# Blocks of 336 instead of 320 columns for four split operands of a two-layer encoder step

## The chip, the cores and the metric

The kernel runs on one core of one Trainium2 chip. The metric is device microseconds of one execution, from the first to the last instruction and what the launch adds around it; the median of a few runs is compared.

## What is computed

Two layers of a streaming encoder are applied to 320 tokens at once (256 of a prompt and 64 of a sample with cached keys), model width 2048. In each layer, with RMS norms in front of each product:

```python
h = rms_norm(x, g_mix);  A, B, C, D = split(h @ w_in)      # four kinds of attention
x = x + concat(A, B, C, D) @ w_out
x = x + square(relu(rms_norm(x, g_mlp) @ w_up)) @ w_down   # 2048 -> 8192 -> 2048
x = x + (ple @ w_ple) * sigmoid(rms_norm(x, g_ple) @ w_ple_gate)
```

All values are float32, and the outputs must keep nearly float32 accuracy.

## The kernel before

Activations are kept feature-major: a tensor of width 2048 is 16 blocks of 128 features (one per partition), and each block holds the 320 tokens as 320 consecutive fp32 words of the partition. `KB` is 16 and `TOK` is 320.

**A product in three matmuls.** The big products run on the fast fp32r form of TensorE, which keeps fewer bits than fp32. Each operand is therefore split in an upper half and a remainder: weights into `whi` and `wlo`, activations into `xhi` and `xlo` (the normed x) or `hhi` and `hlo` (the MLP's activations after the squared relu). The helper `product` (lines 699 to 701) issues lower weight by upper activation, upper by lower, and upper by upper, all into the same PSUM bank:

```python
mm(out, lo[:, k, cols], xh, start=start, stop=False)
mm(out, hi[:, k, cols], xl, start=False, stop=False)
return mm(out, hi[:, k, cols], xh, start=False, stop=stop)
```

The weights are the stationary operand (128 by 128) and the activation block is the moving one (128 by 320). Every matmul therefore has its own weight load.

**Order.** `gemm_chunk` makes four blocks of outputs, a chunk: for 8 units of weights, for 4 output blocks `m`, for the 2 activation blocks `k` of the unit, one `product`. This is 8 x 4 x 2 x 3 = 192 matmuls. A unit is a 512 KB transfer into one of four slots of `ring`; ScalarE copies it to `whi` (line 1136), GpSimd subtracts to get `wlo` (line 662), TensorE waits for `lo_ready`. A layer's MLP is 4 groups of 4 up chunks (from `xhi`, `xlo`) and 4 down chunks (from `hhi`, `hlo`). Ahead of the MLP the last four blocks of `w_out` run the same way (4 times 48 matmuls, on `hhi` and a small tensor `hlast`), behind it `w_ple` (4 times 24 matmuls, on `pleh` and `plel`) and the gate (4 chunks, on `xhi` and `xlo`). VectorE takes the outputs out of PSUM, and makes `xhi` (line 1370), `xlo` (line 1373), `hhi` (line 1766 through the helper of line 1326) and `hlo` (line 1768). Everything else (`w_in`, attention, most of `w_out`) runs ahead of this in a layer, with other tensors. `w_in` has split products too (lines 760 to 763), but there the weights move and the activations are loaded; a unit holds two to four blocks of 256, 264, 288 or 512 weight columns, so that of 264 and of 288 the second block begins 32 and 128 bytes further modulo 256 than the first, and of 256 and 512 at the same place.

**Where the tensors lie.** Buffers are placed by hand in SBUF, many on top of others that are dead by then; all waits are explicit semaphores. A block of 320 words is 1280 bytes, five times 256, so all 16 blocks of a tensor begin at the same place modulo 256 bytes. Worked out from the list of allocations, relative to the first buffer: `xhi`, `hhi`, `whi` and `wlo` begin at 0 modulo 256, `xlo` at 64 (its placement says `+ 64`), `hlo` at 192, `hlast`, `pleh` and `plel` at 32. Weight slots are 4096 bytes and the 128 columns that a matmul loads are 512 bytes, so every weight load begins at 0 modulo 256.

Of the kernel before, what the change touches and what calls it, by code (L numbers as in the profile page):

```python
# [16 lines left out]
TOK = SEQ + DSEQ  # L17
# [6 lines left out]
KB = DM // 128  # L24
# [38 lines left out]
def build(nc, I, O):  # L63
# [4 lines left out]
    with ctx:  # L68
        f32r = mybir.dt.float32r
        top = [nc.sbuf_base + (-nc.sbuf_base) % 64]  # L70

        def sb(name, shape, dtype=f32, at=None):

            words = 1
            for n in shape[1:]:
                words *= n
            if at is None:
                at = top[0]
                top[0] += 4 * (words + (-words) % 8)
            return nc.alloc_sbuf_tensor_at(name, shape, dtype, offset=at)  # L80

        def sem(name):
            return ctx.enter_context(nc.semaphore(name))

        at = top[0]
        x = sb("x", [128, KB, TOK])
        proj_b = sb("proj_b", [128, 3, 1536], at=at)
        early = top[0]
        hid = sb("hid", [128, KB, TOK])
        hhi = sb("hhi", [128, KB, TOK], f32r, early)  # L90
        early += 4 * KB * TOK // 2
        xw = sb("xw", [128, KB, XW], f32r, early)
        xv = sb("xv", [128, KB, 256], f32r, early + 4 * KB * XW)
# [9 lines left out]
        at = top[0]  # L103
# [2 lines left out]
        vtok = sb("vtok", [128, 7, 256])  # L106
        prob = sb("prob", [128, 4, 960])
        probT = sb("probT", [128, 704])
        xhi = sb("xhi", [128, KB, TOK], f32r, at)
        xlo = sb("xlo", [128, KB, TOK], f32r, at + 4 * KB * TOK + 64)  # L110
        assert at + 8 * KB * TOK + 64 <= top[0]
        at = top[0]
        ring = sb("ring", [128, RING, 1024])
        rlo = sb("rlo", [128, RING, 1024], f32r, at)
        at = top[0]
# [6 lines left out]
        eps = sb("eps", [128, 1])  # L122
        at = top[0]
        arena = sb("arena", [128, KB * TOK])
        hlo = sb("hlo", [128, KB, TOK], f32r, at)
        proj_d = arena[:, 0:3 * 1544].rearrange("p (t n) -> p t n", t=3)
        plout = arena[:, :].rearrange("p (b n) -> p b n", b=KB)
        otok = sb("otok", [128, 3, 256])
# [17 lines left out]
        at = top[0]  # L146
# [1725 lines left out]
```

How the kernel before makes its waits and increments, by code:

```python
            def hold(s, value):  # L445
                sp.wait_ge(s, value)
                sp.sem_inc(sp_passed, 1)
# [1 line left out]
            def load(l, q4, u, dst_cols, src, tail=False):  # L450
                s = u % RING
                if tail:
                    sp.wait_ge(lo_ready, l * HL + N_WU + 4 * q4 + u + 1 - TAIL0 - RING)
                else:
                    sp.wait_ge(unit_used, l * UNITS + 4 * q4 + u + 1)
                dst = ring[:, s, 0:dst_cols]
                if len(src.shape) == 3:
                    dst = dst.rearrange("p (a n) -> p a n", a=src.shape[1])
                sp.dma_start(dst, src).then_inc(raw_loaded[s], 16)
# [7 lines left out]
            def first_loads(l):  # L468
                sp.wait_ge(half_free, l * CHUNKS + 2)
                for name, w in VECS:
                    src = I[name][l, :] if name != "lam_init" else I["lam_init"][l, :]
                    sp.dma_start(vec[:, VOFF[name]:VOFF[name] + w], src.partition_broadcast(128)).then_inc(vec_loaded, 16)
                with nc.allow_non_contiguous_dma("feature-major gains"):
                    for i, name in enumerate(("g_mlp", "g_ple")):
                        sp.dma_start(gains[:, 1 + i, :], I[name][l, :].rearrange("(a p) -> p a", p=128)).then_inc(vec_loaded, 16)
                sp.dma_start(flog[:, 0:4, :], I["cache_d_logf"][l, 0, :, :].rearrange("(t p) h -> p t h", p=128))\
                    .then_inc(fc_loaded, 16)
# [29 lines left out]
            def store(g, dst, src):  # L508
                sp.dma_start(dst, src).then_inc(stored[g], 16)
```

## Time and profile before

| | us |
|---|---|
| median of 3 runs | 3526.51 |
| lowest and highest | 3521.68, 3527.46 |
| the profiled execution's own time | 3529.45 |
| its span, first to last instruction | 3527.6 |
| TensorE busy in the span | 3359.4 |

The profiled execution took 3529.45 us, 2.94 us more than the median; 1.85 us of it lie outside the span. Times in the rows are microseconds from the span's start unless marked ns. PE is a matmul on TensorE, PEld a weight load (the two overlap), DVE VectorE, ACT ScalarE, POOL GpSimd. Matmuls are pipelined: a duration of 310 ns is from entry to exit, and what counts is the distance between the starts of two that follow each other. The mean granted TensorE clock is 0.969 of full speed.

### The profile page before, as it was taken

The page shows a single profiled execution, that of the slowest core. Times are in us where ns is not written, and L with a number is a line of the kernel's source. Part 1 is how long each engine was busy: PE and PEld are TensorE (multiplying, and loading weights), DVE is VectorE, ACT ScalarE, POOL GpSimd, SP SyncE. Part 2 cuts the span into 40 slices and gives each one's busy share as a digit, 9 for nine tenths or more (in the row PEclk, how much of TensorE's full clock was granted, in tenths as well). Part 3 has the DMA queues.
Part 4 walks back from the last instruction along what each step waited for, and adds up shares of the span by engine and source line. Part 5 has one row for each costly group of instructions (what it writes and reads, how often), then busy time and mean ns, then how long its engine had stood idle before and what let it go on. Part 6 is the DMA issues. An engine that isn't in the chain of part 4 may idle for free.

```text
span 3527.6 us, 60466 instructions
## 1 busy us (share of the span) xinstructions
PE 3359.4 (95%) x20676; PEld 3030.3 (86%) x20676; DVE 1280.4 (36%) x2301; ACT 1143.7 (32%) x1630; POOL 2261.2 (64%) x2989
## 2 busy tenths in 40 slices
PE   7998989999999999999989998999999999999998
PEld 5676756699999999999967776666999999999998
DVE  4324554464041130324352345445520513204153
ACT  3333332233333333333343332323333333333332
POOL 5554200188888898888865542003988988888886
PEclk9999999899999999999989999989999999999999
DMA  5333322145555455555454333223455554555544
GB/s 159 113 112 110 101 72 87 58 138 150 151 148 153 146 150 153 150 152 148 128 146 114 107 99 109 66 75 94 137 151 152 147 155 139 155 150 149 151 138 125
DMA packets 295723, 453.05 MB, mean 128 GB/s; under 512 B 36336, under 2 KB 111344, under 8 KB 294832
## 3 DMA queue, kind: packets, MB, share of 16 engines
q1 hardware_dynamic: 295328, 448.66, 43.2%
q8 instruction: 179, 2.93, 0.3%
q0 software_dynamic: 144, 0.87, 0.1%
q14 instruction: 72, 0.59, 0.1%
HBM read 435.54 MB, written 14.06 MB: 127 GB/s over the span
## 4 chain that ended last, share of the span: by engine, by line
PE 85%; DVE 6%; issue 4%; DMA 2%; ACT 2%; POOL 1%; SPq 1%; DVEq 0%; ACTq 0%; POOLq 0%
PE ps L700 19%; PE ps L701 19%; PE ps L699 19%; PE ps L797 5%; PE ps L785 5%; PE ps L760 4%; PE ps L763 4%; PE ps L762 3%; PE ps L889 1%; DMA ring<-in_w_in 1%; DVE xhi L1370 1%; PE ps L835 1%; PE ps L893 1%; PE ps L924 1%; PE ps L892 1%
## 5 line engine op out<-in xcount | busy, mean ns | idle before, releaser
L662 POOL TENSOR_TENSOR wlo<-ring,whi 128x256 fp32r<-128x256 f32 x2400 | 1836.5, 801 | 855.5 <-ACT whi L1136 855.0
L1136 ACT ACTIVATE whi<-ring 128x1024 fp32r<-128x1024 f32 x600 | 635.9, 1061 | 1380.6 <-PE ps L701 1380.6
L699 PE MATMUL ps<-xhi,wlo 128*128 128x320 f32 x2560 | 792.8, 310 | 11.2 <-POOL wlo L662 7.2
L700 PE MATMUL ps<-xlo,whi 128*128 128x320 f32 x2560 | 796.6, 311 | 0.0
L701 PE MATMUL ps<-xhi,whi 128*128 128x320 f32 x2560 | 792.9, 310 | 0.0
L701 PE MATMUL ps<-hhi,whi 128*128 128x320 f32 x2176 | 674.0, 310 | 0.0
L699 PE MATMUL ps<-hhi,wlo 128*128 128x320 f32 x2176 | 661.6, 304 | 4.7 <-DVE plel L1746 4.7
L648 POOL TENSOR_TENSOR rlo<-ring,whi 128x256 fp32r<-128x256 f32 (+2 forms) x576 | 421.0, 766 | 368.1 <-ACT whi L1120 367.8
L700 PE MATMUL ps<-hlo,whi 128*128 128x320 f32 x2048 | 629.9, 308 | 0.0
L699 PEld LDWEIGHTS ps<-xhi,wlo 128*128 128x128 f32 x2560 | 486.6, 190 | 14.3 <-issue 12.5
L700 PEld LDWEIGHTS ps<-xlo,whi 128*128 128x128 f32 x2560 | 484.3, 189 | 1.0 <-issue 0.4
L701 PEld LDWEIGHTS ps<-xhi,whi 128*128 128x128 f32 x2560 | 483.4, 189 | 0.0
L699 PEld LDWEIGHTS ps<-hhi,wlo 128*128 128x128 f32 x2176 | 410.4, 189 | 5.3 <-issue 5.1
L760 PE MATMUL ps<-rlo,xw 128*128 128x512 f32 (+3 forms) x1056 | 371.0, 357 | 44.4 <-DVE xw L1339 16.7
L701 PEld LDWEIGHTS ps<-hhi,whi 128*128 128x128 f32 x2176 | 410.2, 189 | 0.0
L1329 DVE TENSOR_TENSOR x<-ps,x 128x320 f32<-128x320 f32 x224 | 107.2, 488 | 797.5 <-PE ps L701 770.2
L700 PEld LDWEIGHTS ps<-hlo,whi 128*128 128x128 f32 x2048 | 383.0, 187 | 0.0
L763 PE MATMUL ps<-whi,xw 128*128 128x512 f32 (+3 forms) x1056 | 362.3, 349 | 0.0
L760 PEld LDWEIGHTS ps<-rlo,xw 128*128 128x128 f32 x1056 | 204.5, 194 | 78.6 <-issue 54.7
L762 PE MATMUL ps<-whi,xv 128*128 128x512 f32 (+3 forms) x704 | 248.0, 352 | 0.0
L785 PE MATMUL ps<-hid,ring 128*128 128x320 f32 x768 | 230.5, 457 | 6.9 <-ACT vtok L1179 3.0
L1120 ACT ACTIVATE whi<-ring 128x1024 fp32r<-128x1024 f32 (+2 forms) x152 | 147.5, 974 | 263.7 <-DMA ring<-in_w_in 223.5
(246 smaller groups left out, 3198.0 us busy)
## 6 DMA issues: line engine op xcount, KB each, us to landing
ring<-in_w_up SPq DMA_DIRECT2D x256, 512.0 KB, 3.7
ring<-in_w_down SPq DMA_DIRECT2D x256, 512.0 KB, 3.8
ring<-in_w_in SPq DMA_DIRECT2D x120, 512.0 KB, 3.6
ring<-in_w_out SPq DMA_DIRECT2D x64, 512.0 KB, 3.8
ring<-in_w_ple_gate SPq DMA_DIRECT2D x64, 512.0 KB, 3.8
xsave<-x SPq DMA_DIRECT2D x8, 640.0 KB, 5.5
x<-xsave SPq DMA_DIRECT2D x8, 640.0 KB, 5.0
ring<-in_w_in SPq DMA_DIRECT2D x16, 288.0 KB, 2.8
```

The costliest lines, as they stand in the source:

```text
L648: last = nc.gpsimd.tensor_tensor(rlo[:, s, c:c + w], ring[:, s, c:c + w], whi[:, s, c:c + w].bitcast(f32), ALU.subtract)
L662: last = nc.gpsimd.tensor_tensor(wlo[:, s, c:c + LO_COLS], ring[:, s, c:c + LO_COLS], whi[:, s, c:c + LO_COLS].bitcast(f32), ALU.subtract)
L699: mm(out, lo[:, k, cols], xh, start=start, stop=False)
L700: mm(out, hi[:, k, cols], xl, start=False, stop=False)
L701: return mm(out, hi[:, k, cols], xh, start=False, stop=stop)
L760: mm(out, head, lo[:, k, :], start=(kk == 0), stop=False)
L762: mm(out, xv[:, kk, t * 128:(t + 1) * 128], hi[:, k, :], start=False, stop=False)
L763: last = mm(out, head, hi[:, k, :], start=False, stop=(kk == KB - 1))
L785: last = mm(ps[:, out_bank(b), 0:TOK], w[:, k - k0, c:c + 128], hid[:, k, :], start=(k == k0), stop=(k == k1 - 1))
L797: return nc.tensor.transpose(out, in_, ident[0:in_.shape[0], 0:in_.shape[0]])
L1120: A(whi[:, s, 0:nk * ncol], ring[:, s, 0:nk * ncol], ACT.Copy).then_inc(hi_ready, 1)
L1136: A(whi[:, s, :], ring[:, s, :], ACT.Copy).then_inc(hi_ready, 1)
```

## The change

A constant `PITCH = TOK + 16` is added, and `xhi`, `xlo`, `hhi` and `hlo` are allocated with blocks of 336 words of which 320 are used. A block is then 1344 bytes, 5 x 256 + 64: each block begins 64 bytes further modulo 256 than the one before it, and every fourth block at the same place. `xlo` moves up with the longer `xhi` and begins again 64 modulo 256; the other three begin where they did. Each tensor is 1024 bytes longer per partition. `x`, `hid`, the weights, `hlast`, `pleh` and `plel`, all instructions, their order, shapes and waits are as they were.

```diff
+        PITCH = TOK + 16
         at = top[0]
         x = sb("x", [128, KB, TOK])
...
-        hhi = sb("hhi", [128, KB, TOK], f32r, early)
+        hhi = sb("hhi", [128, KB, PITCH], f32r, early)[:, :, 0:TOK]
...
-        xhi = sb("xhi", [128, KB, TOK], f32r, at)
-        xlo = sb("xlo", [128, KB, TOK], f32r, at + 4 * KB * TOK + 64)
-        assert at + 8 * KB * TOK + 64 <= top[0]
+        xhi = sb("xhi", [128, KB, PITCH], f32r, at)[:, :, 0:TOK]
+        xlo = sb("xlo", [128, KB, PITCH], f32r, at + 4 * KB * PITCH + 64)[:, :, 0:TOK]
+        assert at + 8 * KB * PITCH + 64 <= top[0]
...
-        hlo = sb("hlo", [128, KB, TOK], f32r, at)
+        hlo = sb("hlo", [128, KB, PITCH], f32r, at)[:, :, 0:TOK]
```

## Rows read from the trace of the kernel before

**Rows 1.** The page, part 1: busy time, share and instructions of each engine.

```profile
PE 3359.4 (95%) x20676; PEld 3030.3 (86%) x20676; DVE 1280.4 (36%) x2301; ACT 1143.7 (32%) x1630; POOL 2261.2 (64%) x2989
```

**Rows 2.** The page, part 4: the chain that ended last, by line.

```profile
PE ps L700 19%; PE ps L701 19%; PE ps L699 19%; PE ps L797 5%; PE ps L785 5%; PE ps L760 4%; PE ps L763 4%; PE ps L762 3%; PE ps L889 1%; DMA ring<-in_w_in 1%; DVE xhi L1370 1%; PE ps L835 1%; PE ps L893 1%; PE ps L924 1%; PE ps L892 1%
```

**Rows 3.** Windows of each layer's split products: length, busy by engine, granted clock, DMA.

```profile
699.45:1769.65 1070.20, 1059.12 (x7218) 1055.94 (x7216) 334.95 (x475) 351.11 (x339) 914.74 (x1196) 0.99 0.50 148
2440.58:3510.40 1069.82, 1058.33 (x7218) 1055.17 (x7216) 334.73 (x475) 351.07 (x339) 915.07 (x1196) 0.99 0.50 146
```

**Rows 4.** The page, part 5: groups of matmuls by operand; count, busy time, mean ns.

```profile
L700 PE MATMUL ps<-xlo,whi 128*128 128x320 f32 x2560 | 796.6, 311 | 0.0
L701 PE MATMUL ps<-xhi,whi 128*128 128x320 f32 x2560 | 792.9, 310 | 0.0
L701 PE MATMUL ps<-hhi,whi 128*128 128x320 f32 x2176 | 674.0, 310 | 0.0
L700 PE MATMUL ps<-hlo,whi 128*128 128x320 f32 x2048 | 629.9, 308 | 0.0
```

**Rows 5.** Timeline of TensorE in a down chunk: start, duration, operands.

```profile
1342.94 0.30 PE L699 MATMUL ps<-hhi,wlo 128*128 128x320 f32 x1
1343.08 0.31 PE L700 MATMUL ps<-hlo,whi 128*128 128x320 f32 x1
1343.22 0.31 PE L701 MATMUL ps<-hhi,whi 128*128 128x320 f32 x1
1343.37 0.30 PE L699 MATMUL ps<-hhi,wlo 128*128 128x320 f32 x1
...
1344.24 0.30 PE L699 MATMUL ps<-hhi,wlo 128*128 128x320 f32 x1
```

**Rows 6.** Tiles hhi and hlo: matmul durations, ns least/median/most.

```profile
L699 PE MATMUL ps<-hhi,wlo x2176: 302/303/615, 699.5 to 3379.2; 128*128 128x320 f32 x198
L701 PE MATMUL ps<-hhi,whi x2176: 304/309/468, 700.1 to 3379.5; 128*128 128x320 f32 x198
L700 PE MATMUL ps<-hlo,whi x2048: 307/308/315, 852.9 to 3379.3; 128*128 128x320 f32 x187
```

**Rows 7.** Windows of whole chunks, TensorE alone: length, busy (count), granted clock, DMA.

```profile
1020.42:1077.03 56.61, 56.61 (x386) 1.00 0.50 149
1638.72:1652.80 14.08, 14.08 (x98) 1.00 0.42 132
...
2536.40:2591.87 55.47, 55.47 (x386) 1.00 0.52 151
...
2759.50:2816.10 56.60, 56.60 (x386) 1.00 0.51 149
2843.89:2927.05 83.16, 83.16 (x578) 1.00 0.52 153
...
3454.90:3510.36 55.46, 55.46 (x386) 1.00 0.33 100
```

**Rows 8.** Windows in w_in's products of 256, 264, 288 and 512 columns, TensorE alone.

```profile
73.36:88.58 15.22, 15.22 (x128) 1.00 0.89 262
345.03:348.56 3.53, 3.53 (x31) 1.00 0.15 24
391.25:400.95 9.70, 9.70 (x75) 1.00 0.38 96
1787.31:1808.86 21.55, 21.55 (x96) 1.00 0.60 151
```

**Rows 9.** The waits: who waited for whom, us in total, times, longest.

```profile
ACT whi L1136 <- PE ps L701: 1380.6, 576, 6.7
POOL wlo L662 <- ACT whi L1136: 855.0, 404, 283.0
```

**Rows 10.** Groups by line and form: VectorE's splitting of x; count, busy, mean ns.

```profile
L1373 DVE SCALAR_TENSOR_TENSOR xlo<-x,gains,xhi 128x320 fp32r<-128x320 f32 x64 | 56.5, 922 | 1.1
L1370 DVE TENSOR_SCALAR xhi<-x,gains 128x320 fp32r<-128x320 f32 x64 | 44.2, 731 | 0.3
```

## The prediction

> **What bounds the kernel now.** I began with the busy times. TensorE works in 3359.4 of 3527.6 us, the next engine, GpSimd, in 2261.2 [rows 1], and the chain that ended last is TensorE's for 85% of the span, with 57% on the three lines of `product`, 699 to 701 [rows 2]. All operands that the change moves are read by these lines, so the windows came next, cut to where they run: 1070.20 us in the first layer and 1069.82 in the second, together 61% of the span, TensorE busy in 99% of it and the granted clock 0.99 [rows 3]. Nothing starves it there. ScalarE's split of the weights waits for TensorE (1380.6 us), and GpSimd waits for ScalarE (855.0 us) [rows 9]. So the stage lasts as long as 7200 matmuls a layer at the pace at which TensorE passes from one to the next, and the question is whether that pace depends on where a moving block begins.
>
> The timeline says that it depends on the operands. In a down chunk three matmuls of one shape, with all data there, start 0.14, 0.14 and 0.15 us after each other, and after three rounds the pattern has moved by 1.30 us, 433 ns a round [rows 5]. Durations give the steps more finely. They are 303 ns for `hhi` with `wlo`, 308 for `hlo`, 309 for `hhi` with `whi` [rows 6]; if the step to the next matmul differs as the duration does, then 3s + 5 + 6 = 433.3, and the steps are about 140.7, 145.7 and 146.7 ns.
>
> Whole chunks show levels. A window's count includes matmuls in flight at its start (two here), so the chunk's own number, 192, is the divisor. Three down chunks: 83.16 us / 576 = 144.4 ns. The last two gate chunks: 55.46 / 384 = 144.4. Two up chunks of the first layer's second group: 56.61 / 384 = 147.4, and of the second layer's second group 56.60, the same; yet two up chunks of the second layer's first group run at 55.47 / 384 = 144.5. `w_ple`, whose halves and blocks all begin at one place modulo 256, takes 14.08 / 96 = 146.7 [rows 7]. The clock is granted at 1.00 in all these, the 2.4 GHz level, and DMA share is no guide (0.33 at 144.4, 0.50 at 147.4). So one program, on one placement, runs at 144.4 in most chunks and at 147.4 in others, and stays on a level for a whole chunk.
>
> For the sum, 14,400 matmuls split as follows. `w_ple` (192) is not moved, and of the rest I put 23 of 74 chunks' worth at 147.4 (the last three up chunks of seven of the eight groups, in which the same windows give 147.4 as in the two shown, and two for the uneven start of the first layer) and 51 at 144.4. The mean is 145.3.
>
> **The change part by part.** It issues the same instructions, waits and DMAs, and no queue is passed. Three things could differ.
>
> TensorE's reads. 2 x 2560 + 2560 + 2 x 2176 + 2048 = 14,080 matmuls read a moved tensor [rows 4]; 1 ns on each is 14.1 us. Of the three steps in a round, two pass between an upper half and its remainder, 64 bytes apart modulo 256. Only the third, from `hhi` of one block to `hhi` of the next, joins places that are equal modulo 256 and will be 64 bytes apart. In the down chunk it is the longest, 146.7 against a mean of 143.2 of the others. Made equal to them it saves 3.5 ns a round, 1.2 ns a matmul, 16 us. The trace has a nearest case of blocks that are offset, in `w_in`. Pace, less one column per cycle of 2.4 GHz: 256 columns 15.22 us / 127 - 106.7 = 13.2 ns, 512 columns 21.55 / 95 - 213.3 = 13.5, both without offset; 264 columns, 32 bytes between blocks, 3.53 / 29 - 110.0 = 11.7; 288 columns, 128 bytes, 9.70 / 73 - 120.0 = 12.9 [rows 8]. Offsetting blocks there gave between 0.3 and 1.8 ns a matmul, 4 to 25 us on 14,080. I take 0.85 ns, 12 us, the lower part of that, because the 264 run is only 29 matmuls long and the round in the down chunk may give back elsewhere what one step saves. The bounds are wider. Below: every step as short as the shortest, 140.7, would give (145.3 - 140.7) x 14,080 = 65 us. Above: every chunk at 147.4 costs 51 x 192 x 3.0 = 29 us.
>
> One rule speaks against any of this. The Trainium skill, "SBUF — State Buffer", section "Who interferes with whom", gives PE two independent read ports (one for the moving operand, one for weight loads) and says that PE and ACT never wait on anyone; by it the place of a block costs nothing and the sum would be 0. The steps of 140.7 to 146.7 ns and the two levels disagree with it, as far as they come from the places; that they do is inferred, not shown. A second page of the Trainium skill, "TensorE: Matmul & The Clock Gate", section "Wait — 56ns, not 53.3ns?", has bf16 matmuls follow each other at N / 2.4 GHz + 2.5 ns, which by an estimate would be 135.8 ns here and 134 us less; no row comes near.
>
> VectorE's and ScalarE's writes into the four tensors. Splitting x takes 56.5 + 44.2 us in all [rows 10], and `xhi` L1370 has 1% of the chain [rows 2], ahead of the first up chunk and the gate. Slices keep 320 consecutive words, so I take 0; a tenth of what is on the chain, 35 us, would be 3.5 us either way. Elsewhere VectorE's idle time (335 of 1070 us busy [rows 3]) covers it.
>
> Overlays. `hlo` now reaches 1024 bytes into `otok`, and `hhi`'s last block onto `kext`; both are used in attention, which is over by then, and no wait was added. Cost 0, and without that cover it would be a wrong value, not time.
>
> Sum: 3529.45 - 12 = 3517.5 for the profiled execution, which lies 2.94 above the median, so 3514.5 by the median, say 3515.
>
> **Rivals.** *Forecast, small gain*: 0.3 to 2 ns a matmul, 3498 to 3522. The upper figure includes that the 147.4 level goes too (23 x 192 x 3.0 = 13 us).
>
> *No change*: only the distance between an upper half and its remainder counts, and it is kept (64 and 192 modulo 256). For it: 264 and 288 columns differ little from 256 and 512. Against: levels change with nothing but what ran before. Time 3520 to 3533. The rule of "SBUF — State Buffer" in the Trainium skill, above, would give the same.
>
> *Slower*: the round of three that settles at 144.4 needs that all blocks begin alike. With the change, places repeat only after six matmuls within a unit (two blocks), and the next unit begins 128 bytes further, so the round is broken at each block. Then the pace is that of `w_ple`, 146.7: 51 x 192 x 2.3 - 23 x 192 x 0.7 = 22.5 - 3.1 = +19 us, 3546; or the upper level, +29, 3556. For it: 147.4 is held through whole up chunks at the same place in both layers, so the good round is not the only one the placement allows. Against: in `w_in` offset blocks never cost more than equal ones. It decides from a mean pace of 145.8, 0.5 ns above now.
>
> *Large gain*: most steps fall towards 140.7, 2.5 ns or more a matmul, 3463 to 3491. For it: that step recurs in every round of the down chunks. Against: no three in a row are so short.
>
> **How the numbers follow.** Chances: small gain 0.36, no change 0.25, slower 0.32, large gain 0.07. This kernel's runs lie within 0.2% of each other (5.8 us of 3526.5), so 0.2%, 7 us, is about what tells a change. Of the small gain a few hundredths end inside that, and as many of "no change" outside, so faster 0.43, same 0.25, slower 0.32. The forecast's own range is 3498 to 3522. For 8 in 10, the range must reach the slower cases up to 3548 (0.10 beyond) and down to 3485 (0.06 beyond).
>
> **What would show it.** Windows on down chunks: 192 matmuls in under 27.7 us for the forecast, 28.2 for the slower rival, 27.0 for a large gain. Up chunks of the middle groups at 27.9 us or less instead of 28.3. In the timeline the third step shorter than now. Stages outside the split products, and the waits of ScalarE and GpSimd per unit, as before. I am wrong if down chunks become slower while up chunks don't move, if the time moves in a stage with no split products, or if VectorE's splits lengthen.

## The result and the profile after

The change costs 16.5 us. Six runs of the kernel before have a median of 3525.26 us (3521.33 to 3533.01), six of the changed kernel 3541.78 (3537.44 to 3546.93): 1.0044 times, with a 95% interval of 1.003 to 1.0059. The profiled execution of the changed kernel took 3546.93 us with a span of 3545.1, 17.5 more than the span before.

The page after, part 1: busy time, share and instructions of each engine. Line numbers after are one higher, so `product` is 700 to 702.

```profile
PE 3374.4 (95%) x20676; PEld 3046.2 (86%) x20676; DVE 1288.5 (36%) x2301; ACT 1143.5 (32%) x1630; POOL 2254.4 (64%) x2989
```

The same instructions run on every engine [rows 1]. TensorE is busy 15.0 us longer, VectorE 8.1; ScalarE and GpSimd are no slower. The same windows of the layers' split products as in [rows 3], in the changed kernel (length, busy by engine, granted clock, DMA share, GB/s):

```profile
699.43:1780.40 1080.97, 1067.65 (x7218) 1064.29 (x7216) 341.17 (x475) 351.16 (x339) 911.79 (x1196) 0.99 0.49 146
2450.83:3528.02 1077.19, 1066.63 (x7218) 1063.73 (x7216) 335.19 (x475) 351.13 (x339) 911.72 (x1196) 0.99 0.49 145
```

They are 10.77 and 7.37 us longer, 18.1 in all. So the whole loss lies here, at the same mean granted clock. TensorE's own work in them is 8.53 and 8.30 us longer; its idle time changes by 2.2 and -0.9 us, so it is not starved either. VectorE is busy 6.2 us more in the first layer and 0.5 in the second, and the first layer's surplus is one instruction. The first of VectorE's 64 splits into `xhi` took 7.55 us, where the longest took 0.91 before (ns least/median/most, first and last start):

```profile
L1371 DVE TENSOR_SCALAR xhi<-x,gains x64: 374/857/7545, 708.2 to 3431.1; 128x320 fp32r<-128x320 f32 x64
```

It ended at 715.8, and GpSimd's first stretch of subtractions ran without a pause from 696.14 to 715.58; that VectorE waited for GpSimd is inferred from this. TensorE then stood idle for 5.01 us before 723.21, the granted clock over 714.53 to 730.34 was 0.78, a part of it at the lower of its two levels, 1.2 GHz (1.00 over the same stretch before), and the first up matmul began 38.0 us into the window instead of 34.2. So some 3.8 of the first layer's 10.77 us are a late start and not pace. One other kernel below has such a split, of 7.67 us: the one with x alone in blocks of 336. In the other fourteen traces none is over 0.96 us. No trace shows whether other executions of the changed kernel have it.

What is longer in ScalarE's and GpSimd's queues is waiting, as the waits after show against [rows 9]:

```profile
ACT whi L1137 <- PE ps L702: 1401.7, 577, 11.2
POOL wlo L663 <- ACT whi L1137: 880.7, 406, 283.6
```

ScalarE waits 21 us longer for TensorE, GpSimd 26 us longer for ScalarE: they stand behind a slower TensorE. Next the windows of whole chunks, TensorE alone, as in [rows 7]:

```profile
1025.73:1081.94 56.21, 56.21 (x387) 1.00 0.50 150
1110.16:1194.72 84.56, 84.56 (x578) 1.00 0.51 150
1648.50:1662.58 14.08, 14.08 (x99) 1.00 0.39 125
...
2547.37:2603.58 56.21, 56.21 (x387) 1.00 0.51 149
2773.30:2829.51 56.21, 56.21 (x387) 1.00 0.51 150
...
3471.70:3528.02 56.32, 56.32 (x386) 1.00 0.32 97
```

Read row by row, divided by the chunks' own matmuls: up chunks of the first layer's second group 56.21 / 384 = 146.4 ns (147.4 before); three down chunks 84.56 / 576 = 146.8 (144.4 before), 28.2 us a chunk, which is the sign that the prediction named for the slower rival; `w_ple`, not moved, 14.08 as before; up chunks of the second layer's first group 146.4 (144.5 before) and of its second group 146.4 (147.4 before); the last gate chunks 56.32 / 384 = 146.7 (144.4 before). Both levels of before are gone. In their place are paces of 146.4 to 146.8, between them and nearer to the upper.

That gives the sum. 32 chunks read `hhi` and `hlo` alone (2048 x 3 / 192): 32 x 192 x 2.4 ns = +14.7 us. 40 read `xhi` and `xlo`; with 21 of them at 147.4 and 19 at 144.4 their mean was 146.0, and 0.4 ns more in 32 up chunks and 0.7 in 8 gate chunks is +2.5 + 1.1 = 3.6 us. Together 18.3, against 16.8 of longer work and 18.1 of longer windows; the split 21 to 19 is an estimate of the prediction, and the windows hold the late start beside the pace.

The timeline of a down chunk after (start, duration, operands), against [rows 5]:

```profile
1120.71 0.31 PE L700 MATMUL ps<-hhi,wlo 128*128 128x320 f32 x1
...
1121.59 0.31 PE L700 MATMUL ps<-hhi,wlo 128*128 128x320 f32 x1
```

Two rounds of three take 0.88 us, 440 ns a round instead of 433. Averaged over the starts of all down chunks in the traces (pauses of 200 ns and more left out), the three steps of a round were 140.2, 145.1 and 148.3 ns; they are 147.5, 147.5 and 145.6. The third is 2.7 ns shorter, as forecast, and the two others are 7.3 and 2.4 longer. The tiles' durations (ns least/median/most) agree, against [rows 6]:

```profile
L700 PE MATMUL ps<-hhi,wlo x2176: 304/310/633, 699.4 to 3395.7; 128*128 128x320 f32 x198
L702 PE MATMUL ps<-hhi,whi x2176: 302/309/468, 700.1 to 3396.0; 128*128 128x320 f32 x198
...
L701 PE MATMUL ps<-hlo,whi x2048: 303/309/318, 856.2 to 3395.8; 128*128 128x320 f32 x187
```

The medians were 303, 309 and 308; they are 310, 309 and 309. The short one of the three is gone. The matmuls became alike, as forecast, but near the length of the long ones.

### The profile page after: what moved, and what is told of

It reads as the page before. It is cut to its first block, busy times and chain, and to the rows that moved or that the text cites. A ratio compares the mean times of both kernels' runs of the same rounds, so it can differ in the third digit from the quotient of the medians.

```text
span 3545.1 us, 60466 instructions
## 1 busy us (share of the span) xinstructions
PE 3374.4 (95%) x20676; PEld 3046.2 (86%) x20676; DVE 1288.5 (36%) x2301; ACT 1143.5 (32%) x1630; POOL 2254.4 (64%) x2989
## 4 chain that ended last, share of the span: by engine, by line
PE 85%; DVE 6%; issue 4%; ACT 2%; DMA 2%; POOL 1%; SPq 1%; DVEq 0%; POOLq 0%; ACTq 0%
PE ps L700 19%; PE ps L701 19%; PE ps L702 19%; PE ps L798 5%; PE ps L786 5%; PE ps L761 4%; PE ps L764 4%; PE ps L763 3%; PE ps L890 1%; DMA ring<-in_w_in 1%; DVE xhi L1371 1%; PE ps L925 1%; PE ps L894 1%; PE ps L836 1%; PE ps L893 1%
## 5 line engine op out<-in xcount | busy, mean ns | idle before, releaser
L700 PE MATMUL ps<-hhi,wlo 128*128 128x320 f32 x2176 | 677.5, 311 | 2.3 <-DVE plel L1747 2.3
```

## The experiments

Places below are bytes modulo 256, relative to where every weight load begins; a pair such as (0, 64) is the place of the upper half and that of the remainder. Before, x lies at (0, 64) and the MLP's activations, h for short, at (0, 192). In the change both run through four places, x through (0, 64), (64, 128), (128, 192), (192, 0), and h through (0, 192), (64, 0), (128, 64), (192, 128).

Three families of causes were set against each other: something other than the places (the longer tensors, their overlays), the distances between the moving blocks, and the place of a moving block against the weight loads that run beside the matmuls. The expectations letter them; here they are told in words. Unless said otherwise, each fence below is that kernel's windows, TensorE alone, and its first two rows are two up chunks (384 matmuls that read x) and three down chunks (576 that read h) of the first layer's second group. The granted clock is 1.00, the 2.4 GHz level, in every one. Each kernel has one traced execution, and its paces are read from that one.

**Blocks 384 words apart, h alone.** 1536 bytes is six times 256, so the tensors get longer than in the change, but all blocks stay at one place. The longer `hhi` reaches 4096 bytes into `kext`, the extended keys, while attention still needs them, so the sample's outputs are not the reference's; this kernel serves for its times alone.

```diff
-        hhi = sb("hhi", [128, KB, TOK], f32r, early)
+        hhi = sb("hhi", [128, KB, TOK + 64], f32r, early)[:, :, 0:TOK]
...
-        hlo = sb("hlo", [128, KB, TOK], f32r, at)
+        hlo = sb("hlo", [128, KB, TOK + 64], f32r, at)[:, :, 0:TOK]
```

> hhi and hlo alone get blocks of 384 words (1536 bytes, six times 256), so they are longer than with the change but still begin at one place modulo 256; xhi and xlo as before. Theory A (the pace follows from where the blocks begin modulo 256): down chunks stay at 144.4 ns a matmul (83.2 us for three), time within 0.2% of before. Rival B (the longer tensors, their overlays or absolute places matter): down chunks near 146.8 ns (84.6 us for three), some 14 us more.

```profile
1018.02:1074.63 56.61, 56.61 (x386) 1.00 0.51 148
1102.40:1185.60 83.20, 83.20 (x578) 1.00 0.51 153
...
1711.83:1767.29 55.46, 55.46 (x386) 1.00 0.47 129
3449.19:3505.80 56.61, 56.61 (x386) 1.00 0.33 97
```

3528.68 us against 3528.01, ratio 1.0007 (0.9996 to 1.0018). Down chunks stay at 144.4 ns, so neither the length nor the overlays slow them. Blocks 1280 and 1536 bytes apart give the same pace, so a step of a whole 256 bytes makes no difference here. The last two rows, gate chunks of the first and of the second layer, are 144.4 and 147.4 ns: the last gate chunks of before ran at 144.4 [rows 7]. x was not touched here, and its level still went from one to the other.

**The change on h alone, and on x alone.** The first:

```diff
+        hhi = sb("hhi", [128, KB, TOK + 16], f32r, early)[:, :, 0:TOK]
...
+        hlo = sb("hlo", [128, KB, TOK + 16], f32r, at)[:, :, 0:TOK]
```

> The change on hhi and hlo alone. Theory A, and rival C (a block pays when it does not begin where the weight loads begin): down chunks at 146.8 ns as with the whole change, up chunks and gate as before (147.4 and 144.4), w_out's last blocks slower too; 32 chunks x 192 x 2.4 ns = +15 us. Rival D (the time of the change came from the x pair): no change.

```profile
1021.67:1077.13 55.46, 55.46 (x386) 1.00 0.51 152
1105.32:1189.88 84.56, 84.56 (x578) 1.00 0.51 150
```

The second:

```diff
+        xhi = sb("xhi", [128, KB, TOK + 16], f32r, at)[:, :, 0:TOK]
+        xlo = sb("xlo", [128, KB, TOK + 16], f32r, at + 4 * KB * (TOK + 16) + 64)[:, :, 0:TOK]
```

> The change on xhi and xlo alone. Theory A and rival C: up and gate chunks at 146.4 to 146.7 ns, down chunks at 144.4. About 21 chunks gain 1.0 ns a matmul (-4 us) and 17 to 19 lose 2.0 to 2.2 (+7 us): +3 us, within 0.2%. Rival D: nearly the whole +17 us is here.

```profile
1029.27:1085.48 56.21, 56.21 (x386) 1.00 0.52 150
1113.25:1196.45 83.20, 83.20 (x578) 1.00 0.52 153
...
1725.98:1782.30 56.32, 56.32 (x386) 1.00 0.45 126
```

On h: 3543.61, ratio 1.0043 (1.0028 to 1.0057), nearly the whole loss, with down chunks at 146.8 as in the full change. On x: 3529.65, ratio 1.0007 (0.9998 to 1.0016), with up chunks at 146.4, gate chunks at 146.7 and down chunks untouched at 144.4. The parts add up to the whole, and x's share is small because it had two levels to lose, one better and one worse. In the first of these kernels x was not moved, and its second group's chunks run at 144.4 (first row), where they ran at 147.4 before; the third group's stay at 147.4.

**The remainder of x at the distance that h has.** x at (0, 192).

```diff
+        xlo = sb("xlo", [128, KB, TOK], f32r, at + 4 * KB * TOK + 192)
```

> The kernel before with xlo 128 bytes further, so that it begins 192 instead of 64 modulo 256 from xhi, as hlo does from hhi. Theory A1 (the distance from upper half to remainder decides which round can settle; 192 settles at 144.4 only): all up chunks at 144.4 ns, about 23 x 192 x 3.0 = 13 us faster than before. Rival E (the level is left over from what ran ahead of the chunk, whatever the distance): the same seven groups hold 147.4, no change.

Here also the third group's up and down chunks:

```profile
1024.10:1080.42 56.32, 56.32 (x386) 1.00 0.51 150
1108.58:1193.05 84.47, 84.47 (x578) 1.00 0.51 151
1251.76:1307.22 55.46, 55.46 (x386) 1.00 0.51 151
1334.96:1418.16 83.20, 83.20 (x578) 1.00 0.51 153
```

A gain was expected and none came: 3532.63, ratio 1.001 (1.0 to 1.002). The second group runs at 146.7 in up and down chunks alike, the third at 144.4 in both. h at (0, 192), which ran at 144.4 wherever it was shown so far, is at 146.6 here without having been moved. So (0, 192) has two levels as well. Here h's level goes with that of the up chunks ahead of it; that what ran ahead decides it is inferred.

**All four tensors moved by 64 bytes.** Every distance between moving blocks is as before; only the weights stay.

```diff
+        hhi = sb("hhi", [128, KB, TOK], f32r, early + 64)
+        xhi = sb("xhi", [128, KB, TOK], f32r, at + 64)
+        xlo = sb("xlo", [128, KB, TOK], f32r, at + 4 * KB * TOK + 128)
+        hlo = sb("hlo", [128, KB, TOK], f32r, at + 64)
```

> All four tensors of the kernel before moved by 64 bytes, blocks of 320, distances between upper half and remainder kept (64 and 192 modulo 256); the weights stay. Theory A (only the places of successive moving blocks against each other count): the levels of before, 144.4 with 147.4 in up chunks. Rival C (the place against the weight loads, which begin at 0, counts): other levels, down chunks above 144.4.

```profile
1022.74:1079.06 56.32, 56.32 (x386) 1.00 0.51 150
1107.65:1193.40 85.75, 85.75 (x577) 1.00 0.49 148
...
3477.62:3533.09 55.47, 55.47 (x385) 1.00 0.33 99
```

3552.2 us (before, beside it, 3524.99), the slowest of all, with down chunks at 85.75 / 576 = 148.9. No block is staggered here. The distances between moving blocks, on which the prediction rested, can't be all that counts. x at (64, 128) has two levels too: 146.7 in nearly all its chunks, and 144.4 in the second layer's last gate chunks (last row).

**Three other pairs of places**, one execution each; before, beside them, is the same 3524.99 us. In turn: x at (0, 128) and h at (0, 64); x at (0, 32) and h at (0, 0); x at (0, 0) and h with blocks of 352 words, which alternate between (0, 192) and (128, 64).

```diff
# x at (0, 128), h at (0, 64)
+        xlo = sb("xlo", [128, KB, TOK], f32r, at + 4 * KB * TOK + 128)
+        hlo = sb("hlo", [128, KB, TOK], f32r, at + 128)
# x at (0, 32), h at (0, 0)
+        xlo = sb("xlo", [128, KB, TOK], f32r, at + 4 * KB * TOK + 32)
+        hlo = sb("hlo", [128, KB, TOK], f32r, at + 64)
# x at (0, 0), h in blocks of 352 words
+        xlo = sb("xlo", [128, KB, TOK], f32r, at + 4 * KB * TOK + 0)
+        hhi = sb("hhi", [128, KB, TOK + 32], f32r, early)[:, :, 0:TOK]
+        hlo = sb("hlo", [128, KB, TOK + 32], f32r, at)[:, :, 0:TOK]
```

> Blocks of 320; xlo 128 from xhi, hlo 64 from hhi modulo 256. Theory A: the distance sets which paces can be held. h at 64 should behave as x did before (144.4 or 147.4, held through whole chunks); x at 128 is not known, between 144.4 and 147.4. Rival E (distance makes no difference, only what ran ahead): the pattern of before by stage, down 144.4.

> Blocks of 320; xlo 32 from xhi, hlo at the same place as hhi modulo 256. Theory A: down chunks at 146.7 ns as in w_ple, where all begin at one place; up and gate chunks at 144.4 or a little above, as w_out's last blocks with hlast at 32 (144.4 and 145.6). Rival E: down chunks at 144.4 as before.

> hhi and hlo in blocks of 352 (128 bytes further each, so two places instead of four), hlo 192 from hhi; x in blocks of 320 with xlo at the same place as xhi modulo 256. Theory A: a step between blocks of any size breaks the round, down chunks at 146 to 147 ns; up and gate chunks at 146.7 without change from chunk to chunk. Rival F (it is the 64 bytes of the change, equal to the distance of the remainder, that hurts): down chunks near 144.4.

The first, 3532.66 us:

```profile
1021.78:1078.10 56.32, 56.32 (x386) 1.00 0.51 148
1105.86:1189.06 83.20, 83.20 (x578) 1.00 0.52 153
```

The second, 3525.63 us:

```profile
1018.99:1074.46 55.47, 55.47 (x386) 1.00 0.51 152
1102.61:1187.09 84.48, 84.48 (x577) 1.00 0.50 151
```

The third, 3539.24 us:

```profile
1018.00:1074.32 56.32, 56.32 (x386) 1.00 0.52 150
1102.48:1186.95 84.47, 84.47 (x577) 1.00 0.51 151
```

(0, 0) costs 146.7 for x and for h alike, and (0, 64) gives h the 144.4 of x's better level; (0, 128) costs 146.7 and (0, 32) 144.4, in some groups 145.5. So it isn't x or h, nor up or down chunks, but the place.

**The change's other places, one per run.** If places against the weight loads decide, the four that the change runs through, each held for whole chunks, must have the change's pace as their mean.

```diff
# all four tensors 128 bytes further: x (128, 192), h (128, 64)
+        hhi = sb("hhi", [128, KB, TOK], f32r, early + 128)
+        xhi = sb("xhi", [128, KB, TOK], f32r, at + 128)
+        xlo = sb("xlo", [128, KB, TOK], f32r, at + 4 * KB * TOK + 192)
+        hlo = sb("hlo", [128, KB, TOK], f32r, at + 128)
# all four 192 bytes further: x (192, 0), h (192, 128): the same lines with 192, 192, 256 and 192
```

> As the run with all four tensors moved by 64 bytes, moved by 128. Theory C2 (the pace of a round is a function of the places of upper half and remainder against the weight loads; the change runs through all four places in turn): the mean over places 0, 64, 128 and 192 is the pace of the change. For the down chunks, 144.4 at 0 and 148.9 at 64 are measured and 146.8 is the change's pace, so places 128 and 192 should have a mean near 146.9. For up chunks, 144.4 to 147.4 at 0, 146.7 at 64, 146.4 the change's pace: mean of the other two near 146.3. Rival A (only the steps between blocks count): down chunks here at one of the levels of before, 144.4.

> Moved by 192 bytes; the fourth place of the four. Theory C2: together with the run at 128 the down chunks' mean is near 146.9 and the up chunks' near 146.3. Rival A: levels of before.

All four tensors at +128, 3545.98 us (before, beside it, 3521.28):

```profile
1019.92:1077.10 57.18, 57.18 (x386) 1.00 0.49 147
1104.99:1188.61 83.62, 83.62 (x577) 1.00 0.51 152
```

At +192, 3540.14 us:

```profile
1018.25:1074.14 55.89, 55.89 (x386) 1.00 0.51 151
1102.51:1187.63 85.12, 85.12 (x577) 1.00 0.50 149
```

By place, each window divided by its matmuls: (128, 192) 148.9, (128, 64) 145.2, (192, 0) 145.5, (192, 128) 147.8. The mean over the change's places of h is (144.4 + 148.9 + 145.2 + 147.8) / 4 = 146.6, and 147.1 with (0, 192) at its upper level; measured 146.8. For x it is (144.4 + 146.7 + 148.9 + 145.5) / 4 = 146.4, 147.1 with (0, 64) at 147.4, and 0.6 less with (64, 128) at its lower level; measured 146.4, and 146.7 in the last gate chunks. The staggered blocks cost about what their places cost one by one, as closely as the two levels let it be told. The blocks of 352 words fit less well: (144.4 + 145.2) / 2 = 144.8, or 145.9 from the upper level, against 146.6 measured. So a step between unlike blocks may cost something beside; that stays open.

**Weights moved too.** All four tensors 64 bytes further, as above, and `whi` and `wlo` as well (with everything that is allocated behind `whi`, `hlo` among it).

```diff
+        hhi = sb("hhi", [128, KB, TOK], f32r, early + 64)
+        wlo = sb("wlo", [128, RING, 1024], f32r, top[0] - 4 * RING * 1024 - 192)
+        xhi = sb("xhi", [128, KB, TOK], f32r, at + 64)
+        xlo = sb("xlo", [128, KB, TOK], f32r, at + 4 * KB * TOK + 128)
...
+        top[0] += 64
         at = top[0]
         whi = sb("whi", [128, RING, 1024], f32r)
```

> As the run with all four activation tensors moved by 64 bytes, and the weight halves whi and wlo moved by 64 bytes too, so that every distance to the weight loads is that of the kernel before while the absolute places are those of that run. Theory C2 (places against the weight loads): the levels of before, down chunks 144.4, up chunks 144.4 or 147.4. Rival G (absolute places modulo 256): the levels of that run, down 148.9, up 146.7.

```profile
1017.81:1074.41 56.60, 56.60 (x386) 1.00 0.50 149
1102.20:1185.39 83.19, 83.19 (x577) 1.00 0.51 153
...
2985.51:3040.98 55.47, 55.47 (x386) 1.00 0.52 151
```

3525.72 us (before, beside it, 3528.94). The moving blocks lie where they cost 148.9, and down chunks are back at 144.4; up chunks show both of x's old levels, 147.4 and 144.4 (last row: the second layer's third group). This is the run that settles it: with the distances between moving blocks and their own places as in the kernel of 148.9, moving the weights brought 144.4 back, in all 32 down chunks (none above 144.7), as all 32 ran at 148.9 there. (What else lies behind `whi` moved too; apart from `hlo`, which was put where it had been in that kernel, these matmuls read none of it.)

The writes of ScalarE into `whi` and of GpSimd into `wlo` moved with them, so they could be what the moving blocks meet. They are not. Here are stretches of the last gate chunk in the kernel with all four tensors at +128, where x lies at (128, 192), and in this one, with all engines as in [rows 3]:

```profile
3517.24:3523.93 6.69, 6.69 (x47) 6.69 (x46) 0.00 (x0) 0.00 (x0) 0.00 (x0) 1.00 0.00 0
3497.95:3503.58 5.63, 5.63 (x41) 5.63 (x40) 0.00 (x0) 0.00 (x0) 0.00 (x0) 1.00 0.00 0
```

VectorE, ScalarE, GpSimd and the DMA engines do nothing in them. Less the two matmuls in flight at the start, 45 take 6.69 us, 148.7 ns each, and 39 take 5.63 us, 144.4. So the difference between the places stands with TensorE's own matmuls and weight loads alone.

**Distances of 32 bytes at other places.** x at (224, 0), h at (32, 0).

```diff
+        hhi = sb("hhi", [128, KB, TOK], f32r, early + 32)
+        xhi = sb("xhi", [128, KB, TOK], f32r, at + 224)
+        xlo = sb("xlo", [128, KB, TOK], f32r, at + 4 * KB * TOK + 256)
+        hlo = sb("hlo", [128, KB, TOK], f32r, at + 64)
```

> Upper halves off the weight loads' place by 32 bytes, remainders at it: xhi at 224, xlo at 0; hhi at 32, hlo at 0. Theory C2 with the order that the other runs suggest (upper half at the loads' place and remainder a little off it is best, the upper half at 64, 128 or 192 costs): both pairs above 144.4, between 144.8 and 148.9. Rival A (only the distance of the halves from each other, here 32 and 224, counts): 144.4 or 145.6 for x, 145.9 for h.

```profile
1021.22:1077.54 56.32, 56.32 (x386) 1.00 0.51 149
1105.70:1190.18 84.48, 84.48 (x578) 1.00 0.51 150
...
1249.49:1306.03 56.54, 56.54 (x387) 1.00 0.50 148
```

3542.54 us. (224, 0) has the distance of (0, 32), which gave 144.4, and costs 146.7, in the third group's up chunks 147.2 (last row); (32, 0) costs 146.7. Distance alone is refuted a second time.

**The rest of the remainder's places, and a better version.** x at (0, 96) and h at (0, 224); and, by itself, x at (0, 32) with h as before.

```diff
# x at (0, 96), h at (0, 224)
+        xlo = sb("xlo", [128, KB, TOK], f32r, at + 4 * KB * TOK + 96)
+        hlo = sb("hlo", [128, KB, TOK], f32r, at + 32)
# x at (0, 32) alone
+        xlo = sb("xlo", [128, KB, TOK], f32r, at + 4 * KB * TOK + 32)
```

> Blocks of 320, xlo 96 from xhi and hlo 224 from hhi modulo 256. No theory has a number; by the places measured (32: 144.4 or 145.6, 64: 144.4 or 147.4, 128 and 0: 146.7) 96 should lie at 144.4 to 147.4 and 224 at 144.4 to 146.7.

> The kernel before with xlo 32 instead of 64 from xhi and everything else as it was. Up and gate chunks at 144.4 or 145.6 as in the run with x at 32, none at 147.4; down chunks at 144.4 if entered well, at 146.7 if h at 192 is entered from x at 32 in its other round. With down at 144.4: 23 x 192 x 2 to 3 ns = 9 to 13 us faster than before. Rival E (what ran ahead decides): no change.

The first, 3541.26 us, 147.0 and 145.9 ns:

```profile
1018.11:1074.56 56.45, 56.45 (x386) 1.00 0.49 149
1102.59:1186.64 84.05, 84.05 (x578) 1.00 0.51 152
```

x at (0, 32) alone; below the two usual rows the third group's up chunks, gate chunks, and both layers' whole windows with all engines:

```profile
1015.23:1070.70 55.47, 55.47 (x386) 1.00 0.52 152
1098.43:1181.63 83.20, 83.20 (x578) 1.00 0.51 153
1240.05:1295.94 55.89, 55.89 (x386) 1.00 0.50 150
1706.45:1761.91 55.46, 55.46 (x386) 1.00 0.44 128
...
696.80:1762.10 1065.30, 1054.29 (x7218) 1050.92 (x7216) 335.11 (x475) 351.14 (x339) 914.51 (x1196) 0.99 0.50 148
2430.69:3496.69 1066.00, 1054.77 (x7218) 1051.48 (x7216) 335.09 (x475) 351.25 (x339) 914.65 (x1196) 0.99 0.49 147
```

3518.16 us against 3521.28, ratio 0.9989 (0.998 to 0.9997): faster than both kernels, by less than expected. No whole chunk of this trace's up and gate products runs at 147.4; some run at 145.5 instead of 144.4. The layers' windows are 4.90 and 3.82 us shorter than in [rows 3], 8.7 us. The medians differ by 3.1 only. The kernel before ran 4 us faster beside this run than in the comparison at the top; why was not found.

## Why the prediction was wrong

The forecast was 3515 us and faster; it is 3541.78, near the slower rival's 3546 and inside the range.

**The step that failed** is "TensorE's reads". It took the third step of a round for long because two equal places meet there, held the two other steps as they were, and priced the gain at 1.2 ns a matmul, then 0.85. The third step did shorten, from 148.3 to 145.6 ns, but the two others went from 140.2 and 145.1 to 147.5, and the round from 433 to 440. The rows had shown that pace depends on operands. What it depends on was read off the moving blocks alone, and the weight load, which each matmul has, was left out: the distances inside a pair were kept, but the pair's place against the weights was not. All four tensors at +64 show it directly, with equal distances and 148.9 ns.

**The nearest case** was not near. Between `w_in`'s 256 and 264 columns [rows 8] the count of columns changes along with the places, and nothing there holds one place and moves the other. It supported the sign of the forecast and gave it its size, and it should have carried only the width of the range.

**The slower rival** had the size: w_ple's 146.7 against 146.8 and 146.4 measured, +19 us against +16.5 by the medians and +17.5 in the span. Its point of decision, a mean pace of 145.8, was passed: weighted by 32 down, 32 up and 8 gate chunks the mean is 146.6. That the size fits is in part luck: `w_ple` lies at (32, 32), a place that the change never visits, and the change's pace comes near it as a mean of others. Its mechanism, a round of three broken at each block, is not what the runs show first: places held for whole chunks, with nothing broken, average to nearly the same. Whether breaking the round adds some tenths, as the blocks of 352 words hint, was not separated.

**No change** fell with the same runs: with all four tensors 64 bytes further the distance inside a pair was kept, and 144.4 ns became 148.9. The rule of the Trainium skill that it leaned on ("SBUF — State Buffer", section "Who interferes with whom") gives the moving operand and the weight load a read port each, independent of one another. If that made them free of each other, the place could not matter; yet 148.9 ns became 144.4 here when the weights followed the moving blocks. No run shows whether a port is where they meet.

**VectorE's splits** were put at 0, with 3.5 us either way as the bound, and their lengthening was named as a sign of being wrong. The sign came up in the trace: one split of 7.55 us and a late start of 3.8 us. It is not what decides the result, since the rest of the windows' 18.1 us is still a loss; the other splits are as long as before (median 857 ns against 861), and the kernel with x alone, whose trace has the same long split, gives 1.0007 over ten executions, with 1 in the interval. Whether the longer blocks bring it about was not tested.

**What held.** The overlays cost nothing that shows: blocks of h at 384 words give 1.0007, with 1 in the interval. `w_ple` kept its 14.08 us. ScalarE and GpSimd only waited longer. The 147.4 level did go, as the upper end of the forecast supposed, but 144.4 went with it, and down chunks, which had been at 144.4 throughout, had nothing to win. That asymmetry stood in [rows 7]: the larger part of the work was at the best level of any whole chunk seen, so spreading it over untried places could hardly help.

## What to carry to other kernels

Where weight loads run beside the matmuls, as here, ask where the moving operand lies modulo 256 against the weights: try one place per run and read whole chunks start to end, and expect of a staggered layout about the mean of its places (here 146.6 to 147.1 by the single places for h, 146.8 measured). Where most of a kernel already runs at the best level that its trace shows, a change that mixes places has more to lose than to win. A stage that runs at two levels on one placement can change level through an edit elsewhere, so compare several groups of it, not one.

## What the runs showed of the hardware

Pace of fp32r matmuls of 128 by 320 with a weight load each, all at a granted clock of 1.00, from the rows above; places against the weight loads, upper half and remainder:

| remainder at | upper half at 0 | upper half elsewhere |
|---|---|---|
| 0 | 146.7 | (32) 146.7; (64) 148.9; (192) 145.5; (224) 146.7 or 147.2 |
| 32 | 144.4 or 145.5 | (32) 146.7, `w_ple` |
| 64 | 144.4 or 147.4 | (128) 145.2 |
| 96 | 147.0 | |
| 128 | 146.7 | (64) 146.7 or 144.4; (192) 147.8 |
| 192 | 144.4 or 146.7 | (128) 148.9 |
| 224 | 145.9 | |

From best to worst it is 4.5 ns in 144.4, 3%, which over 14,080 matmuls would be 63 us. With the upper half at the weights' own place no pair costs more than 147.4. Five pairs were seen at two levels, each held for whole chunks, and for (0, 64) and (0, 192) the level was seen to change with edits to other tensors. A pair that the table gives one level may have another that no trace caught. What in SBUF or TensorE makes a place dear, and what picks the level at entry, was not found.
